# Delta heads of a two-block kernel: squares of 64 with the full contraction and closed together, raw queries, and projection units in the last head's scan

## The reference

```python
q = _l2norm(heads(qkv[..., :A_W], A_DK)) * (A_DK ** -0.5)
k = _l2norm(heads(qkv[..., A_W:2 * A_W], A_DK))
...
sol = lax.linalg.triangular_solve(lhs, rhs, left_side=True, lower=True, unit_diagonal=True)
...
def step(state, inp):
    qk_c, qd_c, kd_c, u_c, w_c, gl_c = inp
    v_new = u_c - jnp.einsum('bhcd,bhde->bhce', w_c, state)
    o = jnp.einsum('bhcd,bhde->bhce', qd_c, state) + jnp.einsum('bhcs,bhse->bhce', qk_c, v_new)
    state = state * gl_c[..., None, None] + jnp.einsum('bhcd,bhce->bhde', kd_c, v_new)
    return state, o
...
o = _rmsnorm(o, norm_g) * jax.nn.silu(z.reshape(bn, s, A_HEADS, A_DV))
return jnp.matmul(o.reshape(bn, s, A_VW).astype(w_out.dtype), w_out)
```

## Time and profile before

| | |
|---|---|
| median of 3 runs | 1777.84 us (1777.79 to 1778.04) |
| profiled execution: own time, span | 1777.21 us, 1775.4 us |
| busy: PE, DVE, ACT, POOL | 1749.8, 1138.1, 808.6, 218.9 us |
| chain that ended last | PE 93% of the span |
| heads 0 to 7 and the last scan | about 206 us to 446 us of the span |

### The profile page before, as it was taken

How to read it: one execution, slowest core, us unless ns; L and a number is a source line. 1 busy time by engine, 2 the same in 40 slices (tenths; PEclk the granted TensorE clock), 3 DMA queues, 4 the chain that set the end, 5 groups by cost and what they waited for, 6 DMA issues and landing times.

```text
span 1775.4 us, 26333 instructions
## 1 busy us (share of the span) xinstructions
PE 1749.8 (99%) x10352; PEld 1440.3 (81%) x10352; DVE 1138.1 (64%) x1643; ACT 808.6 (46%) x1366; POOL 218.9 (12%) x216
## 2 busy tenths in 40 slices
PE   8999999999999999999999999999999999999999
PEld 6888777777789988888887887889988888876677
DVE  4776487878588755667431587788746766433763
ACT  4433555554245753324453454236643354434541
POOL 2001133331000000010000153000010000101600
PEclk9999999999999999999999999999999999999999
DMA  5233100000323344343232100333354353430002
GB/s 165 89 91 104 48 14 14 1 1 2 95 89 102 96 145 152 107 137 95 72 95 72 57 16 1 95 96 115 100 190 135 102 164 91 152 97 24 25 1 71
DMA packets 103276, 147.23 MB, mean 83 GB/s; under 512 B 5153, under 2 KB 71153, under 8 KB 102912
## 3 DMA queue, kind: packets, MB, share of 16 engines
q1 hardware_dynamic: 96192, 121.45, 21.7%
q0 software_dynamic: 6976, 24.27, 4.2%
HBM read 143.61 MB, written 2.10 MB: 82 GB/s over the span
## 4 chain that ended last, share of the span: by engine, by line
PE 93%; DVE 3%; issue 1%; ACT 1%; DMA 1%; SPq 0%; DVEq 0%; ACTq 0%
PE bk L302 23%; PE bk L300 23%; PE bk L301 23%; PE bk L1209 2%; PE bk L1188 2%; PE bk L1198 1%; PE bk L3339 1%; PE bk L3340 1%; PE bk L1243 1%; PE bk L2475 1%; PE bk L3361 1%; PE bk L1269 1%; PE bk L1225 1%; PE bk L1081 1%; PE bk L1103 1%
## 5 line engine op out<-in xcount | busy, mean ns | idle before, releaser
L279 DVE TENSOR_TENSOR wlo<-raw,whi 128x1024 fp32r<-128x1024 f32 x166 | 199.5, 1238 | 280.4 <-ACT whi L273 280.0
L300 PE MATMUL bk<-act_hi,whi 128*128 128x512 f32 (+1 forms) x880 | 324.1, 368 | 0.3 <-DVE wlo L783 0.3
L301 PE MATMUL bk<-act_lo,whi 128*128 128x512 f32 (+1 forms) x880 | 321.0, 365 | 0.0
L302 PE MATMUL bk<-act_hi,wlo 128*128 128x512 f32 (+1 forms) x880 | 320.8, 365 | 0.0
L302 PE MATMUL bk<-whi,act_lo 128*128 128x512 f32 (+1 forms) x776 | 306.8, 395 | 0.0
L300 PE MATMUL bk<-whi,act_hi 128*128 128x512 f32 (+1 forms) x776 | 305.7, 394 | 0.5 <-DVE act_lo L632 0.5
L301 PE MATMUL bk<-wlo,act_hi 128*128 128x512 f32 (+1 forms) x776 | 303.7, 391 | 0.0
L273 ACT ACTIVATE whi<-raw 128x1024 fp32r<-128x1024 f32 x166 | 168.8, 1055 | 264.3 <-PE bk L302 244.2
L300 PEld LDWEIGHTS bk<-act_hi,whi 128*128 128x128 f32 x880 | 165.7, 188 | 31.4 <-DVE wlo L783 0.9
L301 PEld LDWEIGHTS bk<-act_lo,whi 128*128 128x128 f32 x880 | 165.9, 188 | 29.6 <-issue 1.0
L302 PEld LDWEIGHTS bk<-act_hi,wlo 128*128 128x128 f32 x880 | 165.8, 188 | 29.4
(11 more groups left out here) (453 smaller groups left out, 3013.4 us busy)
## 6 DMA issues: line engine op xcount, KB each, us to landing
raw<-in_mlp_w SPq DMA_DIRECT2D x100, 512.0 KB, 4.4
raw<-in_a_w_in SPq DMA_DIRECT2D x32, 512.0 KB, 4.0
work<-in_mlp_w SPq DMA_DIRECT2D x28, 512.0 KB, 4.4
work<-in_w_mod POOLq DMA_DIRECT2D x24, 512.0 KB, 3.9
raw<-in_b_w_in SPq DMA_DIRECT2D x24, 512.0 KB, 3.9
raw<-in_w_in SPq DMA_DIRECT2D x14, 512.0 KB, 4.1
raw<-in_a_w_out SPq DMA_DIRECT2D x8, 512.0 KB, 3.7
raw<-in_b_w_out SPq DMA_DIRECT2D x8, 512.0 KB, 3.7
```

The source lines that it names most:

```text
L279: nc.vector.tensor_tensor(wlo[b][:, hs], src[hf][:, :], whi[b][:, hs], ALU.subtract).then_inc(w_ready, 1)
L300: nc.tensor.matmul(acc, lhs_hi, rhs_hi, start=first, stop=False, skip_group_check=True)
L301: nc.tensor.matmul(acc, lhs_hi, rhs_lo, start=False, stop=False, skip_group_check=True)
L302: return nc.tensor.matmul(acc, lhs_lo, rhs_hi, start=False, stop=last, skip_group_check=True)
```

## The change

1. **Squares of 64.** Open and close read all 128 rows (`[:, c, r]` in place of `[r, c, r]`): the same 64 columns by 64, the other half of the rows being zero for them. The two squares of a chunk then share their rows and differ in their columns. At levels 1 to 3 the close is in one piece, and the scan's read and state stand ahead of it (level 1) or behind it (levels 2 and 3).
2. **Raw queries.** The queries aren't normed: `pe_a_norm` runs for keys alone, and `dve_a_query` is gone. The query's sum of squares is needed for the output's epsilon only: ScalarE squares the raw query (scaled), GpSimd adds it to the squares of the output (`pool_a_out_add`), and `pe_a_out_sum` sums both. That sum moves from behind the close of level 4 into level 5, and ScalarE's log of it behind `act_a_row_exp`. `pe_a_rows` for direction 1 moves behind the transposes of the values, into `bk[6]`. In the last head the four products by decayed rows move from VectorE to GpSimd.
3. **The last scan.** The 16 units (three matmuls each) of `a_out`'s half 0, slab 0 stand between the steps of the last scan (`fill`), token tile 3 in `bk[4]`. The other 16 follow by feature tile, `k` outside and `st` inside, with the output sum after two of them. Half 1's token tile 0 uses `bk[3]`.

```diff
+        def sum_bank(name, half, st):
+            if name == "a_out" and (half, st) in ((0, 3), (1, 0)):
+                return bk[(4, 3)[half]]
+            return bk[4 * half + st]
...
-                        mm = nc.tensor.matmul(bk[s][r, at:at + n], a_keys(h)[r, c, r], z_right(h, l, c * P + r.start, n, r),
+                        mm = nc.tensor.matmul(bk[s][r, at:at + n], a_keys(h)[:, c, r], z_right(h, l, c * P + r.start, n),
...
-                        mm = nc.tensor.matmul(level_sum(l, s)[r, at:at + r.stop - r.start], A["X"][r, c, r], A["T"][r, c, r],
+                        mm = nc.tensor.matmul(level_sum(l, s)[r, at:at + r.stop - r.start], A["X"][:, c, r], A["T"][:, c, r],
...
-                mm = nc.tensor.matmul(bk[7][:, cs], a_kn(h)[:, cs], A["qn"][:, cs], start=True, stop=True, skip_group_check=True)
+                mm = nc.tensor.matmul(bk[7][:, cs], a_kn(h)[:, cs], a_qkvT[:, h, cs], start=True, stop=True, skip_group_check=True)
...
-                if l == 4 and h > 0:
-                    pe_a_out_sum(pe, h - 1)
                 if l == 5:
                     pe_a_value_turn(pe, h)
-                    if more:
-                        pe_a_norm(pe, h + 1, 1)
+                    pe_a_rows(pe, h, 1)
...
+            fill(2)
             pe_a_scan_new(pe, h, 0)
             for cc in range(1, ST):
+                fill(1)
                 pe_a_scan_read(pe, h, cc)
                 pe_a_scan_state(pe, h, cc)
+                fill(1)
                 pe_a_scan_solve(pe, h, cc)
+                fill(2)
                 pe_a_scan_new(pe, h, cc)
+            fill(len(first_slab))
+            for k in (4, 5, 6, 7):
+                for st in range(ST):
+                    mm = pe_a_out_unit(pe, k, st)
+                    if (k, st) == (4, 1):
+                        pe_a_out_sum(pe, h)
+                    if k == 7:
+                        mm.then_inc(sum_ready if st < 3 else slab_used, 1)
...
+            nc.scalar.activation(A["sq"][:, 1, :], a_qkvT[:, h, :], ACT.Square, scale=P * RMS_EPS ** 0.5)
...
-            nc.scalar.activation(A["rs"][:, 1, :], bk[7][:, :], ACT.Ln, bias=RMS_EPS, scale=1.0 / P).then_inc(G["o_ln"], 1)
+            nc.scalar.activation(A["rs"][:, 1, :], bk[7][:, :], ACT.Ln, bias=P * RMS_EPS * 1e-6, scale=1.0 / P).then_inc(G["o_ln"], 1)
...
+            pool.wait_ge(G["o_sq"], h + 1)
+            nc.gpsimd.tensor_tensor(act_f[:, h, :], act_f[:, h, :], A["sq"][:, 1, :], ALU.add).then_inc(G["o_add"], 1)
```

More of the change, by code:

```diff
@@ L382, in pe_token_last, with pe_token_layer @@
                 between(pe, b, st)
-        def pe_token_layer(pe, name, between, middle=None, first=None, order=range(ST)):
+        def pe_token_layer(pe, name, between, middle=None, first=None, order=range(ST), halves_of=(0, 1)):
             pairs = PH[name][1] // 4
-            for half in range(2):
+            for half in halves_of:
                 pair0 = half * pairs
@@ L828, in pe_a_in @@
                     pe_feature_slab(pe, "a_in", k2, b)
-            for i in range(2):
-                pe_a_norm(pe, 0, i)
+            pe_a_norm(pe, 0)
             pe_a_decay(pe, 0)
@@ L1018, in a_first @@
         def a_first(h):
[L1019 removed]
+            return A["qd1"] if h == 0 else chunks(a_qkvT[:, 16, :])
         def a_decay(h):
@@ L1072, in kk_bank, with pe_a_norm @@
             return 7 if h > 0 else 4
-        def pe_a_norm(pe, h, i):
-            if h > 0 and i == 0:
+        def pe_a_norm(pe, h):
+            if h > 0:
                 pe.wait_ge(G["vn"], 8 * (h - 1))
[L1078 to L1081, removed]
+            pe.wait_ge(G["l2_sq"], h + 1)
+            nc.tensor.matmul(bk[5][:, :], ones[:, :], A["sq"][:, 0, :], start=True, stop=True).then_inc(G["l2_sum"], 1)
         def pe_a_kk(pe, h):
-            pe.wait_ge(G["qkn"], 2 * h + 1)
+            pe.wait_ge(G["qkn"], h + 1)
             if h > 0:
-                pe.wait_ge(G["row_exp"], 2 * h)
-            else:
+                pe.wait_ge(G["pt"], h)
+            if h > 1:
+                pe.wait_ge(G["o_ln"], h - 1)
+            if h == 0:
                 pe.wait_ge(G["dec_exp"], 1)
@@ L1199, in pe_a_level_open, with pe_a_level_close @@
                 mm.then_inc(G["turned_y"], 1)
-        def pe_a_level_close(pe, h, l, parts=(0, 1)):
-            for s in parts:
+        def pe_a_level_close(pe, h, l):
+            for s in range(2):
                 pe.wait_ge(G["x"], 12 * h + 2 * (l - 1) + s + 1)
@@ L1339, in pe_a_last, with fill @@
         def pe_a_last(pe):
             h = AH - 1
+            first_slab = [(k, st) for k in range(4) for st in range(ST)]
+            def fill(n):
+                for _ in range(n):
+                    k, st = first_slab.pop(0)
+                    mm = pe_a_out_unit(pe, k, st)
+                    if not first_slab:
+                        mm.then_inc(slab_used, 1)
+            fill(2)
             pe_a_scan_new(pe, h, 0)
             for cc in range(1, ST):
+                fill(1)
                 pe_a_scan_read(pe, h, cc)
@@ L1599, in dve_a_head @@
                         dve_a_query_decay(dve, h, 0)
-                if l == 1 and h > 0:
-                    dve_a_query(dve, h)
                 if l == 4 and h > 1:
                     dve_a_out(dve, h - 2)
-                if l == 6 and not more:
-                    dve_a_query_decay(dve, h, 0)
         def dve_a_last(dve):
@@ L1678, in pool_a_head, with pool_a_query_decay @@
                 pool_a_unit(pool, h + 1)
+            else:
+                for d in range(2):
+                    pool_a_query_decay(pool, h, d)
+        def pool_a_query_decay(pool, h, d):
+            pool.wait_ge(G["row_exp"], 2 * h + d + 1)
+            nc.gpsimd.tensor_tensor(A[f"ke{d}"], A[f"qd{d}"], a_kn(h).rearrange("p (c s) -> p c s", c=ST), ALU.mult).then_inc(G["ke"], 1)
+            pool.wait_ge(G["ke"], 2 * h + d + 1)
+            nc.gpsimd.tensor_tensor(A[f"qd{d}"], A[f"qd{d}"], chunks(a_qkvT[:, h, :]), ALU.mult
+                                    ).then_inc(G["qd"], 1)
         def gap(eng):
```

167 lines of the change are left out of this document (78 added, 89 removed).

## The result

| | before | after |
|---|---|---|
| median | 1777.94 us (1777.79 to 1778.33) | 1767.87 us (1767.71 to 1768.13) |
| profiled execution: own time, span | 1777.21, 1775.4 us | 1768.13, 1766.3 us |
| busy PE, DVE, POOL | 1749.8, 1138.1, 218.9 us | 1736.0, 1132.2, 234.8 us |

The ratio is 0.9942, 95% interval 0.9929 to 0.9954. The granted clock is 1.00 in both traces. Lines 1209, 1188, 1198 and so on of before are 1206, 1185, 1195 after; VectorE's add to `Z` is L1595, the masks of `T` L1579, the output sum L1278.

What follows compares the result with a forecast made beforehand. TensorE was taken to bound the kernel, busy 29.4 of 29.5 us in middle heads. 32 us from the heads plus 4 from the last scan, 36 off 1777.2, gave 1742 us with the median's 0.6; range 1734 to 1753.

Steps and rivals of the forecast that it cites:

- This form empties nothing: Heads' squares: 128-row, 64-column form removes all 13 visits (changes to squares and back), 0.35 us each, 4.55 a head.
- Rival 1: Heads' squares: they run side by side, but each visit still costs 0.35 us; 16 us gained, 1761; chance 0.12.
- Side by side: Squares sharing their rows in opens and closes still run in parallel, 0.03 us a record, so no added cost.
- rival 2: Heads' squares: no visits, but one square after the other, 0.057 us a record; 8.3 us gained, 1769; chance 0.22.
- rival 3: Opens and closes, levels 1 to 5: squares' weights not loaded under preceding matmuls; slower, up to 1835 us; chance 0.08.
- Closes in one piece: Closes of levels 1 to 3: nothing more if visits are free, otherwise 0.33 us less, three times a head.
- The norm of the queries: In each of 8 heads, dropping it saves 0.86 us of TensorE.
- the output sum's move: Between close of level 4 and open of level 5: a 0.5 us wait for VectorE's add, charged in every head.
- GpSimd's addition: In the heads: 1.0 to 1.6 us more GpSimd work, cost 0 as results are needed 8 us later; uncovered, 1.3 a head.
- 0.6 a head for VectorE's order: At a head's start VectorE's operations add to more than TensorE's: 0.6 us charged, between 0 and 1.5.
- The last scan: Last head's scan: 16 units fill 5.5 us of free time, gain 4.6 us, bounds 0 and 5.5.
- 0.6 given back: After the last scan: VectorE late for the layer norm by up to 1.2 us, 0.6 charged, leaving 4.0 gained.

Runs made afterwards that it cites:

- e5: The kernel before with only the closes of levels 1 to 3 in one piece: 1770.79 us, ratio 0.9957.
- e1: The changed kernel with the squares in their old form, 64 rows by 64 columns: 1767.26 us, ratio 0.9944.
- e6: The changed kernel with the left square multiplied twice, the right left out, so all squares stand in columns 0 to 63: 1796.92 us in one execution.
- e12: The changed kernel with the second block's 72 matmuls of 128x64 reading plain float32 instead of float32r: 1793.25 us in one execution, beside 1779.31 for before.
- e4: The changed kernel with GpSimd's two unit matrices for the next head moved ahead of the addition and the masks: 1762.89 us, ratio 0.9917.
- e9: e4 with the decayed rows of direction 0 moved between the close of level 4 and the open of level 5: 1760.75 us, ratio 0.9898.
- e2: The changed kernel without GpSimd's addition, the query's part of the output's epsilon left out: 1762.17 us, ratio 0.9918.
- e3: The changed kernel with the output sum back behind the close of level 4, GpSimd's addition kept: 1765.78 us, ratio 0.9935.
- e8: The changed kernel with all 16 units behind the last head's scan, none between its steps: 1770.91 us, ratio 0.9958.

## Why the prediction was right or wrong

**"This form empties nothing. That takes away all 13 visits, 4.55 us a head."** Wrong, and it is most of the miss: 1.0 of 4.55 came, by the closes (e5), and nothing by the form (e1). Rival 1's mechanism is what happened. The step that failed was the transfer from the earlier trace rows. I weighed that those rows have only the left columns; that wasn't the difference (e6). They are float32r rows, and the squares are plain float32 (e12). The column of shapes says f32 for both; the program tells the type, and so does the number of records, one for a float32r matmul and two for a float32 one. The Trainium skill, TensorEngine Tiling (Array Packing), Tiling Modes, says that a change of mode drains the engine. The heads, e6 and e12 agree with it at 0.35 us a visit, and the earlier trace rows, with float32r operands, do not. I gave it 12% on the strength of rows that weren't of the same kind; the measured price of a visit in the very loop, which I had just worked out, ought to have weighed more.

**Side by side.** Right. Squares that share their rows take 0.03 a record, as before; one after the other 0.063 (e6), against my 0.057. So rival 2 and rival 3 were both wrong: with all 128 rows in use, loads still run beside matmuls, even in one place (0.063 and not 0.11), where the rule quoted for rival 3 would not have had it.

**Closes in one piece, 0.33 each if visits cost.** Right: 0.34 (e5).

**The norm of the queries, 0.86, and the output sum's move.** With e5's 28.5 and e4's 28.1 they are worth 0.4 a head together. The prediction's numbers for this case (0.86 - 0.26) give 0.6. From the starts, the other 0.2 is in two places. The output sum takes 0.95 in its new place, 335.33 to 336.28, with squares behind it, and I had taken 0.86. And the rows of direction 1 now stand between forms of 128 rows instead of ahead of squares, which costs another 0.1. No run tested either apart. The wait of 0.5 behind the close of level 4 came as charged (0.98 from close to open), and was what e9 had to win.

**GpSimd's addition: "Cost 0".** Wrong. The cover that I named (its results are needed 8 us later) is real, and in the windows of the heads none of its consumers was late. I counted only who waits for GpSimd, not who works beside it. With the output sum in its new place it cost about 5 us: 1.03 in each of five heads, and 4.3 and 4.4 us by the ratios of e2 and e4. With the sum in its old place the wait is 0.23 (e3). The rows that could have warned me stand in the trace before, VectorE's product L1542 twice and GpSimd's scales beside the second:

```profile
342.48 0.68 DVE L1542 TENSOR_TENSOR work<-work 128x512 f32<-128x512 f32 x1
...
344.47 1.44 DVE L1542 TENSOR_TENSOR work<-work 128x512 f32<-128x512 f32 x1
```

```profile
344.32 1.05 POOL L1639 TENSOR_TENSOR work<-work 128x512 f32<-128x512 f32 x1 [2.47 <-PE bk L1198]
```

**0.6 a head for VectorE's order, between 0 and 1.5.** That the heads lost about as much is luck. The loss is the same 1.03 us in five heads, not a second one; I had put it at a head's start and for VectorE's order, and it came at the end and from GpSimd. In e4, where VectorE is at 22.2 us, close to my 22.3, TensorE's only long wait in a middle head is the 0.5 charged separately.

**The last scan, 4.6, and 0.6 given back.** 5.4 and 1.1. The sum of 4.0 for both is near the 4.3 measured, but of other parts, so that is luck: I had the units fill 5.5 us of idle time. 2.4 of that disappeared because VectorE's queue in the scan became shorter, by the four products and by splits in another order, for which I had credited nothing, and only the rest was there to fill (e8). The give-back was inside its bound of 1.2; most of it is the wait at L435, whose size of 1.0 stays open, since other runs with the same units have 0.4 or 0.5.

**The sum.** By the heads' starts in the two traces: ahead of the heads 0.8, head 0 0.25, head 1 1.4, heads 2 to 6 2.1, head 7 0.7, the scan 5.4, the transition -1.1. Together 9.5, against 9.1 us between the spans. Rival 1 had the squares right. Its 16 us off the median of before are 1762, where the prediction says 1761; with the 5 us of GpSimd on top it would have been 1767, one under the measured 1768.

## What to carry to other kernels

- Rows that show a form free of charge are evidence for the same operand type only. Look up what the type is in the program before a row from another stage outweighs a price measured in this one.
- Work moved to an idle engine is not free because its result is needed late. Lay the timelines of GpSimd and VectorE beside each other, and put GpSimd's work where VectorE reads PSUM or waits.
- When several short pieces of a special form stand apart, bringing them together gains as many visits as there are fewer pieces; the shape inside a piece may gain nothing (e5 and e1).

## What the runs showed of the hardware

- A visit to a tile of 64 columns among 128x128 ones costs 0.35 us with float32 operands, in 64x64 (e1) and in 128x64, for one place (e6) and for two; with float32r operands of the same tile, in one place, nothing.
- Two float32 matmuls of 128x64, in columns 0 to 63 and 64 to 127, run side by side: 0.03 us a record, 0.063 if all are in one place (e6).
- A VectorE `TENSOR_TENSOR` of 128x512 with both operands in SBUF, 0.68 us alone, takes up to 1.54 beside GpSimd's (L1555 of the change); with one operand in PSUM it stays at 0.68 (L1517). GpSimd's pair of products takes 2.05 alone and 2.96 beside VectorE's (L1689 of the change).
